# Attention low parts in full 128-row tiles, small tensors moved into dead buffers

## The reference, cut to what matters

```
logits = einsum('bhqd,bhkd->bhqk', q, k) * SCALE + bias      # NSA selected, NSA window, MoBA
logits = einsum('bhtd,bhmd->bhtm', q, mk) * SCALE            # memory heads
p = softmax(logits);  o = p @ v
```

## Time and profile before

| | us |
|---|---|
| median of three runs | 476.09 |
| lowest and highest of them | 475.78, 476.2 |
| span of the profiled execution, first to last instruction | 475.1 |
| PE busy in it | 457.9 |
| DVE, ACT, POOL busy in it | 276.3, 241.2, 46.1 |

### The profile page before, as it was taken

How to read it: one execution, slowest core, us unless ns; L and a number is a source line. 1 busy time by engine, 2 the same in 40 slices (tenths; PEclk the granted TensorE clock), 3 DMA queues, 4 the chain that set the end, 5 groups by cost and what they waited for, 6 DMA issues and landing times.

```text
span 475.1 us, 5965 instructions
## 1 busy us (share of the span) xinstructions
PE 457.9 (96%) x2096; PEld 360.3 (76%) x2096; DVE 276.3 (58%) x476; ACT 241.2 (51%) x412; POOL 46.1 (10%) x79
## 2 busy tenths in 40 slices
PE   3999999989999999999999998999999999999995
PEld 3776889967767777777787867888888888888884
DVE  2673893787455554645388595655555555544443
ACT  4563943475655545445445466754445554534421
POOL 4030000002111111111170041000000000000000
PEclk9999999989999999999999999999999999999998
DMA  8899724253342223243274545755566555555302
GB/s 285 308 381 322 238 53 175 88 178 94 127 134 90 88 89 93 88 144 120 89 284 135 196 138 169 231 177 181 181 196 193 193 196 186 177 178 177 90 0 88
DMA packets 50880, 77.79 MB, mean 164 GB/s; under 512 B 2068, under 2 KB 27372, under 8 KB 50856
## 3 DMA queue, kind: packets, MB, share of 16 engines
q1 hardware_dynamic: 49272, 73.07, 46.9%
q0 software_dynamic: 1424, 4.34, 2.7%
q10 hardware_dynamic: 160, 0.07, 0.1%
HBM read 76.40 MB, written 1.07 MB: 163 GB/s over the span
## 4 chain that ended last, share of the span: by engine, by line
PE 90%; DVE 3%; ACT 2%; DMA 2%; issue 1%; POOL 0%; POOLq 0%; SPq 0%; DVEq 0%; ACTq 0%
PE acc L1097 25%; PE acc L1099 23%; PE acc L1098 23%; PE sbank L1268 3%; PE sbank L1267 3%; PE ob L1344 3%; PE ptb L1318 2%; DMA mems<-in_mem 2%; PE ob L1251 1%; PE ob L1346 1%; PE ptb L1423 1%; ACT wh L455 1%; PE ob L1333 1%; DVE wl L724 1%; DVE gates L934 1%
## 5 line engine op out<-in xcount | busy, mean ns | idle before, releaser
L724 DVE TENSOR_TENSOR wl<-raw,wh 128x1024 fp32r<-128x1024 f32 (+1 forms) x130 | 158.6, 1227 | 84.2 <-ACT wh L455 83.5
L455 ACT ACTIVATE wh<-raw 128x1024 fp32r<-128x1024 f32 (+1 forms) x130 | 135.3, 1046 | 94.7 <-PE acc L1099 87.1
L1097 PE MATMUL acc<-wh,xh 128*128 128x512 f32 (+1 forms) x384 | 154.9, 403 | 0.2 <-DVE xl L754 0.2
L1099 PE MATMUL acc<-wh,xl 128*128 128x512 f32 (+1 forms) x384 | 149.2, 389 | 0.0
L1098 PE MATMUL acc<-wl,xh 128*128 128x512 f32 (+1 forms) x384 | 149.0, 388 | 0.0
L1097 PEld LDWEIGHTS acc<-wh,xh 128*128 128x128 f32 x384 | 72.4, 189 | 17.5 <-issue 1.4
L1099 PEld LDWEIGHTS acc<-wh,xl 128*128 128x128 f32 x384 | 72.4, 189 | 15.2
L1098 PEld LDWEIGHTS acc<-wl,xh 128*128 128x128 f32 x384 | 72.6, 189 | 13.5 <-issue 0.5
L408 POOL TENSOR_SCALAR sx<-sx,jst 128x256 f32<-128x256 f32 (+1 forms) x48 | 20.2, 433 | 173.4 <-DVE jst L975 98.6
L1097 PE MATMUL acc<-wh,ah 128*128 128x512 f32 x88 | 34.9, 397 | 0.0
L1099 PE MATMUL acc<-wh,al 128*128 128x512 f32 x88 | 34.8, 396 | 0.0
(11 more groups left out here) (214 smaller groups left out, 463.2 us busy)
## 6 DMA issues: line engine op xcount, KB each, us to landing
raw<-in_w_in SPq DMA_DIRECT2D x20, 1024.0 KB
raw<-in_w_ffn_gate SPq DMA_DIRECT2D x22, 512.0 KB
raw<-in_w_ffn_up SPq DMA_DIRECT2D x22, 512.0 KB
raw<-in_w_ffn_down SPq DMA_DIRECT2D x22, 512.0 KB
raw<-in_w_mix_out SPq DMA_DIRECT2D x4, 1024.0 KB
bp<-g_scratch SPq DMA_DIRECT2D x1, 2304.0 KB, 8.5
raw<-in_w_nsa_o SPq DMA_DIRECT2D x2, 1024.0 KB
raw<-in_w_in SPq DMA_DIRECT2D x2, 560.0 KB
```

Source lines behind the costliest of these rows:

```text
L455: nc.scalar.activation(wh[:, k, :, 0:w], raw[:, slot, 2 * half:2 * half + 2, 0:w], ACT.Copy).then_inc(hi_done, 1)
L724: nc.vector.tensor_tensor(wl[:, k, :, 0:w], raw[:, slot, 2 * half:2 * half + 2, 0:w], wh[:, k, :, 0:w].bitcast(F32), ALU.subtract).then_in ...
L1097: nc.tensor.matmul(bank[:, 0:w], h[:, k, c], wh[:, slot, s, 0:w], start=first, stop=False)
L1099: return nc.tensor.matmul(bank[:, 0:w], l[:, k, c], wh[:, slot, s, 0:w], start=False, stop=last)
```

## The change

`klo` gets a tile of 128 rows for each of the 12 key heads. POOL zeroes all of it at the start, and `low_qk` writes the low part of a head into the half of its side, so the other half stays zero. L1268 then multiplies all 128 rows of `qst` by all 128 rows of `klo`; the q low rows meet zeros. `klo` grows from 6 to 12 KB in each partition. To make room `hx`, `hidk` and `hidv` move into the space of `memh`, and `vcz` and `pcz` become views of `pat`. They can no longer be zeroed at the start: POOL zeroes `hidv` after the fourth sub is multiplied, `vcz` after batch 3 is transposed and `pcz` after batch 6. VectorE waits on `zeroed` in four places instead of one.

```diff
-            klo = sb("klo", [P, K_HEADS // 2, SEQ], F32R, s)
+            klo = sb("klo", [P, K_HEADS, SEQ], F32R, s)
...
         with ExitStack() as s:
             gcmp = sb("gcmp", [P, 2, PAIRS, GROUPS * NCMP], F32, s)
+            hx = sb("hx", [P, 3, 4 * NCMP], F32, s)
+            hidk = sb("hidk", [P, GROUPS * NCMP], F32, s)
+            hidv = sb("hidv", [P, GROUPS, HPG, 32], F32, s)
...
-            pcz = sb("pcz", [P, TILES, GROUPS, HPG, 32], F32, s)
+            c_km = C_KM - SLICE
+            pcz = pat[:, :, c_km:c_km + GROUPS * HPG * 32].rearrange("p t (g i c) -> p t g i c", g=GROUPS, i=HPG)
...
-            vcz = sb("vcz", [P, GROUPS, HPG, HD], F32, s)
+            vcz = pat[:, :, 0:HPG * HD].rearrange("p g (i d) -> p g i d", i=HPG)
...
# POOL
-            nc.gpsimd.memset(hidv[:], 0.0).then_inc(zeroed, 1)
-            nc.gpsimd.memset(vcz[:], 0.0).then_inc(zeroed, 1)
-            nc.gpsimd.memset(pcz[:], 0.0).then_inc(zeroed, 1)
+            nc.gpsimd.memset(klo[:].bitcast(F32), 0.0).then_inc(zeroed, 1)
             nc.gpsimd.memset(ckeys[:].bitcast(F32), 0.0).then_inc(zeroed, 1)
             pool.wait_ge(bp_d, 16)
...
+            pool.wait_ge(mm_done, 4)
+            nc.gpsimd.memset(hidv[:], 0.0).then_inc(zeroed, 1)
+            pool.wait_ge(qk_pe, QK_COMPRESS + 1)
+            nc.gpsimd.memset(vcz, 0.0).then_inc(zeroed, 1)
+            pool.wait_ge(qk_pe, QK_LAST)
+            nc.gpsimd.memset(pcz, 0.0).then_inc(zeroed, 1)
             for n, (kind, *_r) in enumerate(jobs):
...
# VectorE, low_qk
-                        high, dst = khh[rows, heads, :], klo[rows, pairs, :]
+                        high, dst = khh[rows, heads, :], klo[rows, heads, :]
...
+            dve.wait_ge(zeroed, 1)
             low_qk(0)
...
-            dve.wait_ge(zeroed, 4)
+            dve.wait_ge(zeroed, 3)
             for i in range(HPG):        # writes hidv
...
+            dve.wait_ge(zeroed, 4)
             for i in range(HPG):        # writes vcz
...
+                    dve.wait_ge(zeroed, 5)
                     for t in range(TILES):        # writes pcz, in slot 2
...
# TensorE
-            def logits(dst, q, side, t, high, low):
+            def logits(dst, q, t, high, low):
                 cols = slice(P * t, P * t + P)
                 nc.tensor.matmul(dst, qst[:, q, cols], high, start=True, stop=False)
-                return nc.tensor.matmul(dst, qst[half_rows(side), q, cols], low, start=False, stop=True)
+                return nc.tensor.matmul(dst, qst[:, q, cols], low, start=False, stop=True)
...
-                    ins = logits(sbank[:, n % 2, c0:c1], q, side, t, khh[:, k, 0:c1 - c0], klo[half_rows(side), k // 2, 0:c1 - c0])
+                    ins = logits(sbank[:, n % 2, c0:c1], q, t, khh[:, k, 0:c1 - c0], klo[:, k, 0:c1 - c0])
```

More of the change, by code:

```diff
@@ L86, in job_plan @@
     for m in range(MOBA_H):
-        jobs.append(("moba", m, Q_MOBA + m, m % 2, K_MOBA + m, NSA_H + m))
+        jobs.append(("moba", m, Q_MOBA + m, K_MOBA + m, NSA_H + m))
     for m in range(MEM_H):
-        jobs.append(("mem", m, Q_MEM + m, m % 2, K_MEM + m, None))
+        jobs.append(("mem", m, Q_MEM + m, K_MEM + m, None))
     for h in range(NSA_H):
         for kind, first in (("sel", K_SEL), ("win", K_WIN)):
-            jobs.append((kind, h, Q_NSA + h, h // HPG, first + h // HPG, h))
+            jobs.append((kind, h, Q_NSA + h, first + h // HPG, h))
     return jobs
@@ L195, in build_layer @@
             post = sb("post", [P, 2, CMP_LEN], F32, s)
-            pcz = sb("pcz", [P, TILES, GROUPS, HPG, 32], F32, s)
+            c_km = C_KM - SLICE
+            pcz = pat[:, :, c_km:c_km + GROUPS * HPG * 32].rearrange("p t (g i c) -> p t g i c", g=GROUPS, i=HPG)
             w2k = sb("w2k", [CMP_HID, 2, HD], F32, s)
             w2v = sb("w2v", [CMP_HID, HD], F32, s)
-            hx = sb("hx", [P, 3, 4 * NCMP], F32, s)
-            hidk = sb("hidk", [P, GROUPS * NCMP], F32, s)
-            hidv = sb("hidv", [P, GROUPS, HPG, 32], F32, s)
             ckeys = sb("ckeys", [P, GROUPS, 2, 16], F32R, s)
-            vcz = sb("vcz", [P, GROUPS, HPG, HD], F32, s)
+            vcz = pat[:, :, 0:HPG * HD].rearrange("p g (i d) -> p g i d", i=HPG)
             xc = sb("xc", [P, TILES, NSA_H, 16], F32, s)
@@ L284, in stacked @@
             h0 = first + second * side
-            return slice(h0, h0 + step + 1, step), slice(h0 // 2, h0 // 2 + 2)
+            return slice(h0, h0 + step + 1, step)
         def qk_bank(beta):
@@ L533, in high_qk @@
                 for side in range(2):
-                    heads, _pairs = stacked(beta, side)
+                    heads = stacked(beta, side)
                     if QK_BATCHES[beta][0] == "q":
@@ L821, in low_qk @@
                     rows = half_rows(side)
-                    heads, pairs = stacked(beta, side)
+                    heads = stacked(beta, side)
                     if QK_BATCHES[beta][0] == "q":
@@ L942, in _ @@
                 if n < JOBS:
-                    kind, h, _qb, _qh, _kb, bh = jobs[n]
+                    kind, h, _q, _k, bh = jobs[n]
                     dve.wait_ge(s_done, n + 1)
@@ L1296, in scores @@
             def scores(n):
-                kind, h, q, side, k, _bh = jobs[n]
+                kind, _h, q, k, _bh = jobs[n]
                 if n == 0:
```

## The result

The changed kernel takes 458.08 us, the median of four runs (457.53 to 458.28), against 476.14 us for four runs of the kernel before in the same comparison. The ratio is 0.9621, 95% interval 0.9607 to 0.9634: 18.06 us less, where 16.7 were forecast (459.4, range 457.3 to 462.6). Two executions of later kernels were slow (1542.96 us in experiment 1, 489.68 us in experiment 6) and are left out of every median and ratio here.

The account below looks back on a forecast made before the run. The job loop was taken as bound by TensorE's back-to-back work. Twenty jobs at 0.68 us and four memory heads at 0.79 save 16.7 us, other edits cost 0: 476.1 - 16.7 = 459.4 us, range 457.3 to 462.6.

Parts of the forecast that it names:

- The main step: Logits in the job loop: full rows in L1268 save 0.68 us per job, 0.79 per memory head, 16.7 us in all.
- second sum: Logits with the Trainium skill's shorter steps: 0.75 us saved per job, 0.83 per memory head, 18.3 in all, ending at 457.8.
- Rivals 2 and 3: Logits: weight loads stay in the open, 467.9 us, 3%; or the gap is not the rows' and stays, 476.1 us, 3%.
- Rival 4: Job loop: a late engine opens waits in each slot and the clock falls, making the kernel slower, 481.8 us with eight; 2%.
- the clock: After the idle before job 0: a stretch near 1.2 GHz may vanish or come once more, 1.7 us either way.
- The reserve in job 1: Job 1, POOL's end to TensorE's transposes: 1.99 us before the change, of which 1.3 us remain after it.
- a wait for POOL in the loop: Sign in the profile after: TensorE waiting for POOL in the job loop would make the prediction wrong.
- Rival 1: Seven tight job slots: VectorE's lateness of 0.39 us reaches TensorE, 2.7 us lost, 462.1 us; 6%.
- The other edits: Zeroing of `klo`, `hidv`, `vcz`, `pcz` and added DVE waits: cost 0 each, at most 0.6 us loss.
- Zeroing `klo`: POOL at the start: 6 x 0.55 = 3.3 us, done near 8.3 us, cost taken as 0.

Follow-up runs that it names:

- experiment 1: The changed kernel with the low-key logit matmul back on 64 rows, padded layout, zeroing and waits kept: 476.10 us, ratio 1.0005 to the kernel before.
- experiment 6: The kernel of experiment 5 with one VectorE split of a weight piece put behind the merge of the NSA branch: 450.98 us, ratio 0.9465.
- experiment 3: The changed kernel with both logit matmuls on 64 rows, leaving out low queries by high keys: 464.12 us in one run.
- experiment 5: The changed kernel with value products on 128 weight columns instead of 64, odd heads writing the bank's other half: 451.45 us, ratio 0.9482.

## Why the prediction was right, and where it was off

**The main step held, in mechanism and in size.** The cost of the four switches of rows was read from the distances of weight loads, and it is shown by undoing the step, by doing it alone, and by moving all logits to 64 rows, where the three inner gaps go. That the array empties in such a gap is the explanation; the rows show only the gap. Steps after the change are 0.11 and 0.12, as taken (0.108 and 0.119). The Trainium skill, TensorEngine Tiling (Array Packing), section Key Properties, says that changing the tiling mode, not the tile, drains the engine; experiments 1, 3 and 5 agree and put the price here, 0.15 us for a switch of rows behind 128 columns and 0.20 behind 256, and 0.34 us for what experiment 5 changes in a slot. The prediction's second sum, 457.8 us, came nearer to the measured time than its forecast, but by luck: it took 0.75 us saved in a job, and the rows show 0.67.

**Three readings of the prediction were off.** It calls 6.4 and 1.5 us TensorE's two longest waits; the same view has one of 1.7 us for POOL behind the loop, which the change leaves as it was. It numbers jobs one too low from job 6 on. And it measures the reserve in job 1 to the row of the transposes, 112.07, while the load, which is what waits, stands at 111.85, so 1.8 us and not 1.99. None of them enters the sum.

**Rivals 2 and 3 fell.** Loads run under the matmul ahead of them on the very same rows (0.11 apart, and 0.12 with 256 columns, where a load and its columns one behind the other would make 0.23). By the rule of the Trainium skill, TensorE: Matmul & The Clock Gate, The mechanism, a load would overlap only on other rows; the rows here differ from it, and the measurement decides. Rival 4 did not come.

**The term that was mis-sized is the clock.** The prediction held the stretch near 1.2 GHz after job 0 for something that may vanish or come once more, 1.7 us either way, and left it out of the middle. Its reason was that TensorE's wait of 1.5 us before job 0 stays. It does stay (1.5 us in every profile), and the stretch goes all the same: with 64-row logits behind that wait it comes in most executions, with 128-row logits in none of the profiles. Where it comes it costs 1.43 us by the starts in the kernel before, 5.84 - 3.83 - 0.68 = 1.33 with job 0 alone and 5.63 - 3.83 - 0.20 = 1.60 in experiment 3, against the 1.7 that the prediction read from the clock column; the median with jobs 1 to 23 lies 2.15 - 0.68 = 1.5 below the one with all jobs, and the mean span with job 0 alone only 1.4 - 0.68 = 0.7 above the changed kernel's. As it comes in 19 of 23 executions of the kernel before, it is worth some 1.2 us on average, an estimate, and with it the forecast is about 458.2, against 458.08 measured. That is nearly all of the 1.3 us, though the interval of the ratio leaves 0.6 us either way. That the stretch hangs on the rows in job 0 is shown. No run takes the wait away, so what the wait has to do with it is not shown; only that the 64-row jobs 1 to 23, which follow no wait, bring no stretch. Whether the idle gaps inside that job do it, or 64-row matmuls as such, is not: in experiment 3 three of the four gaps were gone and it came still.

**The reserve in job 1 was over-estimated, by the same step.** 1.3 us were to remain between POOL and the transposes of job 1. TensorE got there another 1.4 us sooner, as the clock did not fall, while VectorE had only its 1.39 us of waiting to gain, and the reserve ran out (timeline after, beside the earlier trace rows):

```profile
106.75 0.83 POOL L412 TENSOR_SCALAR sx<-sx,jst 128x128 f32<-128x128 f32 x2 [3.16 <-DVE jst L981]
...
107.63 0.31 PEld L1325 LDWEIGHTS ptb<-const,sx 128*128 128x128 f32 x3 [0.40 <-POOL sx L412]
```

POOL ends at 107.58. From the start of the last matmul ahead of the load (107.26) to the next logits (108.90) it is 1.64 us, where it is 1.44 for the same jobs in the kernel before and in the next slot here, so 0.20 us are lost once. With 64 rows in job 0 alone, where the clock fell, the same way takes 1.44 and there is no such wait. The prediction named a wait for POOL in the loop as a sign against it; this one is there, small. Rival 1, VectorE's lateness in the seven tight slots, costs nothing: before job 18 it now starts its additions without a wait, behind L998, and TensorE's slots from slot 2 on stay at 4.5 to 5.0 us.

**The other edits cost nothing,** as costed: a ratio of 1.0005 in experiment 1, which has them all. Zeroing `klo` took 2.68 us instead of 3.3 and was over at 7.6 us:

```profile
4.96 2.68 POOL L394 MEMSET klo<- 128x3072 f32 x1
```

## What to carry to other kernels

Where TensorE is bound, read the distances between weight loads, form by form: a small matmul between large ones that differs from them in rows or in weight columns can cost more than its columns do. Filling it up with zeros, or with neighbours whose results are ignored, cost nothing in the stream here; experiment 5 shows the price behind it, more instructions for the engines that copy the valid halves out. When TensorE then gets faster, look at the reserves of the engines it feeds, and remember that a clock that no longer falls spends them too.

## What was not expected of the hardware

- The lower clock after job 0 came when a wait of 1.5 us was followed by 64-row matmuls (profiles of four kernels; 0.50 to 0.55 in the lowest stretch of 2 us) and stayed away with the same wait and 128-row matmuls (five kernels, 1.00).
- A 64-row stream of matmuls with 128 weight columns runs at the same 0.10 to 0.12 us per step as a 128-row stream.
- At the start the step between equal matmuls goes from 0.43 to 0.23 us at 12.1 us into the span in one execution and at 14.9 in another, with the same instructions of TensorE up to there. The 1.03 us between the profiles of before and after come from this, 0.2% of this kernel.
